# Gathering the dilated patterns' outputs in six transfers instead of 24, and a key projection moved among the fills of the last dilated pass

## What is computed

```python
y_a = dense_attention(...)        # A: latent attention, 4 heads
y_b = dense_attention(...)        # B: grouped-query attention
for gi, (w, r) in enumerate(((128, 1), (512, 4), (2048, 16))):
    o, lse = dilated_group(cq5[:, :, gi], ck5[:, :, gi], cv5[:, :, gi], r, w // (2 * r), dil_bias[gi])
    outs.append(o); lses.append(lse)
alpha = softmax(stack(lses), axis=0)
y_c = sum(alpha[..., None] * stack(outs), axis=0)     # C: dilated, 3 patterns combined per position
y_d = banded_attention(d_q, d_k, d_v, 128, 128, win_bias, sink)   # D: windowed
y = concatenate([y_a, y_b, y_c, y_d]) * silu(gate_path)
x = x + sum(sigmoid(merge_logits) * (y per branch @ w_branch), axis=2) @ w_out
```

## Time and profile before

| | us |
|---|---|
| median of three runs | 2906.52 (2903.6 to 2906.72) |
| the profiled execution | 2898.05 |
| its span, first to last instruction | 2895.9 |
| PE busy | 2720.7 (94%) |
| DVE busy | 1310.1 (45%) |
| ACT busy | 1022.5 (35%) |
| POOL busy | 724.5 (25%) |
| chain that ended last, PE's share | 83% |
| mean granted TensorE clock | 0.98 of full speed |

### The profile page before, as it was taken

How to read it: one execution, slowest core, us unless ns; L and a number is a source line. 1 busy time by engine, 2 the same in 40 slices (tenths; PEclk the granted TensorE clock), 3 DMA queues, 4 the chain that set the end, 5 groups by cost and what they waited for, 6 DMA issues and landing times.

```text
span 2895.9 us, 36963 instructions
## 1 busy us (share of the span) xinstructions
PE 2720.7 (94%) x13836; PEld 2240.9 (77%) x13836; DVE 1310.1 (45%) x2815; ACT 1022.5 (35%) x2085; POOL 724.5 (25%) x449
## 2 busy tenths in 40 slices
PE   7899999999999989999879999998999999899996
PEld 6677887878888768877776777787888887688875
DVE  3575366522434355523145734585234444455222
ACT  4464116412444425511135631173024443354012
POOL 2100331033434232222220014301333333222231
PEclk9999999999999999999989999999999999999998
DMA  7000210021111221112050011100212113111122
GB/s 241 27 1 10 55 43 19 1 59 45 47 44 41 75 72 30 37 46 95 23 183 15 1 28 46 42 10 10 64 40 52 40 40 103 37 37 37 44 95 80
DMA packets 204194, 146.00 MB, mean 50 GB/s; under 512 B 21688, under 2 KB 187192, under 8 KB 203976
## 3 DMA queue, kind: packets, MB, share of 16 engines
q1 hardware_dynamic: 190188, 137.08, 16.7%
q10 hardware_dynamic: 13824, 6.49, 0.8%
HBM read 124.44 MB, written 27.49 MB: 52 GB/s over the span
## 4 chain that ended last, share of the span: by engine, by line
PE 83%; DVE 9%; ACT 3%; issue 2%; DMA 1%; POOL 1%; SPq 1%; ACTq 0%; POOLq 0%; DVEq 0%; another core or an unknown queue 0%
PE ps L892 21%; PE ps L855 9%; PE ps L856 9%; PE ps L857 9%; PE ps L998 5%; PE ps L1023 4%; PE ps L955 4%; PE ps L956 4%; PE ps L957 4%; PE ps L1071 3%; PE ps L1039 3%; PE ps L1008 2%; DVE pt_slots L1814 2%; PE ps L1000 1%; DVE nm L1650 1%
## 5 line engine op out<-in xcount | busy, mean ns | idle before, releaser
L2051 POOL CAST wh<-wraw 128x1024 fp32r<-128x1024 f32 (+2 forms) x162 | 176.2, 1088 | 2058.8 <-PE ps L857 873.1
L855 PE MATMUL ps<-xh,wh 128*128 128x512 f32 x1120 | 442.1, 395 | 3.0 <-ACT pt_split L1542 2.2
L856 PE MATMUL ps<-xl,wh 128*128 128x512 f32 x1120 | 438.2, 391 | 0.0
L857 PE MATMUL ps<-xh,wl 128*128 128x512 f32 x1120 | 438.1, 391 | 0.0
L2053 POOL TENSOR_TENSOR wl<-wraw,wh 128x1024 fp32r<-128x1024 f32 (+2 forms) x162 | 421.0, 2599 | 13.0
L892 PE MATMUL ps<-xh,wh 128*128 128x512 f32 x864 | 353.9, 410 | 3.1 <-ACT att L1368 1.2
L892 PE MATMUL ps<-xh,wl 128*128 128x512 f32 x864 | 344.4, 399 | 0.0
L892 PE MATMUL ps<-xl,wh 128*128 128x512 f32 x864 | 344.2, 398 | 0.0
L855 PEld LDWEIGHTS ps<-xh,wh 128*128 128x128 f32 x1120 | 212.3, 190 | 47.5 <-ACT pt_split L1542 3.0
L857 PEld LDWEIGHTS ps<-xh,wl 128*128 128x128 f32 x1120 | 211.7, 189 | 44.7
L856 PEld LDWEIGHTS ps<-xl,wh 128*128 128x128 f32 x1120 | 212.1, 189 | 43.2
(11 more groups left out here) (213 smaller groups left out, 4748.1 us busy)
## 6 DMA issues: line engine op xcount, KB each, us to landing
wraw<-in_w_in_dram SPq DMA_DIRECT2D x128, 512.0 KB, 3.9
xres<-acc SPq DMA_DIRECT2D x2, 4096.0 KB, 15.8
toep<-toep_row SPq DMA_DIRECT2D x32, 256.0 KB, 10.7
wraw<-in_w_branch_dram SPq DMA_DIRECT2D x64, 128.0 KB, 3.9
wraw<-in_w_out_dram SPq DMA_DIRECT2D x16, 512.0 KB, 3.7
acc<-xres SPq DMA_DIRECT2D x16, 512.0 KB, 7.7
dil_out<-cst ACTq DMA_DIRECT2D x96, 66.0 KB, 1.6
att<-dil_out SPq DMA_DIRECT2D x48, 132.0 KB, 2.5
```

What stands on the lines that cost most here:

```text
L855: pe.matmul(dst, ah, bh, start=i == 0, stop=False)
L856: pe.matmul(dst, ah, bl, start=False, stop=False)
L857: last = pe.matmul(dst, al, bh, start=False, stop=i == len(ks) - 1)
L2051: inc(pool.tensor_copy(high, raw), w_hi)
```

## The change

The dilated outputs now lie as (pattern, block, head) in `dil[0]`, in `att`, and `dil[1]`, a second buffer `dil_late` over the memory of the old query stacks. `load_groups_outputs(half, groups)` moves one pattern's half in one transfer (528 KB), with a semaphore for each half. Two transfers, patterns 0 and 1 of half 0, are issued at the start of the last pass, after 64 of the 96 stores; the four others after all stores, with no wait for `yn_set`. The two fills of the key projection join the gate fills of the last pass: 8 matmuls a step, and 4 in each of the four steps of the tail. PE's other fills of branch D are put around the transposes in another order, with other banks.

```diff
-        dil = att[:, 0:4 * GROUPS * HEADS * REC].rearrange("p (t g h f) -> p t g h f", t=4, g=GROUPS, h=HEADS)
+        dil = [a.rearrange("p (g t h f) -> p g t h f", g=GROUPS, t=4, h=HEADS)
+               for a in (att[:, 0:4 * GROUPS * HEADS * REC], dil_late[:, :])]
...
-        GATE_PART = 7
+        GATE_PART = 8
+        TAIL_PART = 4
...
-                            fill_bank.append((0, 1, 2, 3, 6, 7)[i % 6])
+                            fill_bank.append((2, 3, 0, 1, 6, 7)[i % 6])
...
-                def load_groups_outputs(half):
-                    for st in range(half * 4, half * 4 + 4):
-                        for g in range(GROUPS):
-                            load(dil[:, st % 4, g, :, :].rearrange("p h f -> p (h f)"),
-                                 dil_out[g, st * P:(st + 1) * P, :], dil_in)
+                def load_groups_outputs(half, groups):
+                    for g in groups:
+                        load(dil[half][:, g, :, :, :].rearrange("p t h f -> p t (h f)"),
+                             dil_out[g, half * HALF:(half + 1) * HALF, :].rearrange("(t p) f -> p t f", p=P), dil_in[half])
...
-                for t in dilated["gate_tiles"] + windowed_tiles[:4]:
+                for t in dilated["gate_tiles"]:
+                    load_tile(t)
+
+                sp.wait_ge(lg_ready, dil_passes[5]["units"][0])
+                for s in dil_stored:
+                    sp.wait_ge(s, DIL_PER_SLOT * 16 * 4 // 6)
+                load_groups_outputs(0, (0, 1))
+                for t in windowed_tiles[:4]:
                     load_tile(t)
...
-                load_groups_outputs(0)
+                load_groups_outputs(0, (2,))
+                load_groups_outputs(1, (2, 0, 1))
                 sp.wait_ge(exp_done, c_u1)
                 load_bias(3)
-                sp.wait_ge(yn_set, 1)
-                load_groups_outputs(1)
...
-                        for j, t in enumerate(p["tiles"][:3]):
+                        def dilated_y(half):
+                            pe.wait_ge(yn_set, half + 1)
+                            for st in range(half * 4, half * 4 + 4):
+                                y_transposes(branches[2]["y"][st], yc[:, half, st % 4, :])
+
+                        for j, t in enumerate(p["tiles"]):
+                            if j == 0:
+                                continue
                             pe.wait_ge(w_split, t + 1)
                             for half in range(2):
                                 fill(p["fill"] + 2 * j + half, t, half)
-
-                        for st in range(ST):
-                            pe.wait_ge(yn_set, st // 4 + 1)
-                            y_transposes(branches[2]["y"][st], yc[:, st // 4, st % 4, :])
+                                if j == 2 and half == 0:
+                                    dilated_y(0)
+                        dilated_y(1)
...
-                                    fills_part(b["gate_fill"], b["gate_tiles"], GATE_PART * i, GATE_PART * (i + 1))
+                                    fills_part(b["gate_fill"], b["gate_tiles"] + keys_tile, GATE_PART * i, GATE_PART * (i + 1))
+                            if n == 2 and s >= u1:
+                                m = GATE_PART * 16 + TAIL_PART * (s - u1)
+                                fills_part(b["gate_fill"], b["gate_tiles"] + keys_tile, m, m + TAIL_PART)
```

More of the change, by code:

```diff
@@ L1874, in _ @@
                         windowed = branches[3]["passes"][0]
+                        for f in range(windowed["fill"], windowed["fill"] + 2):
+                            stack_rests(windowed, f)
                         for half in range(2):
-                            dve.wait_ge(dil_in, 16 * 4 * GROUPS * (half + 1))
+                            dve.wait_ge(dil_in[half], 16 * GROUPS)
                             if half:
```

38 lines of the change are left out of this document (20 added, 18 removed).

## The result

The changed kernel took 2862.2 us (median of four runs, 2860.3 to 2865.1), the kernel before in the same rounds 2905.1 (2901.4 to 2906.7): ratio 0.9855, interval 0.9838 to 0.9872, 42.9 us faster. The changed kernel's profiled execution took 2860.8, the one before 2898.05, so the two profiles can explain 37.2 us.

What follows compares the result with a forecast made beforehand. PE was taken to bound the kernel, busy 94% of the span. Gains of 17.7 and 17.0 us less 2 x (0.5 + 1.6 + 0.3) gave 30 off 2898.05, so 2868; plus 8.5, 2876.5 us, range 2865 to 2894.

Steps and rivals of the forecast that it cites:

- Lock-steps: At the y transposes, two groups of four instead of one of eight: 0.3 us lost a layer.
- the same stop and 0.6: Layer 1 gains as layer 0: the 9.4 us stop, and 0.6 us for three low-clock fill matmuls behind it.
- so PE waits 1.6 us: At the first y, PE asks at 1018.3 and the combination ends at 1019.9: a 1.6 us wait in each layer.
- The split's price: POOL's split of the values' tile beside the first combination costs DVE 2.7 us on top of 8.8 alone.
- the 0.6 for a key copy: The first of POOL's eight key copies may catch one more sum of the first combination, adding 0.6 us.
- The offset: The timed median, 2906.52, lies 8.5 us above the profiled execution; the same was added to the changed kernel's 2868.
- The late first combination: Rival: DVE held up by POOL or shared DMA engines, first y 5.5 us later; 8 us a layer, 2892.5; chance 0.13.
- The low clock: Rival: after the first y's wait, 168 matmuls stay at the low clock, 33 us a layer lost; 2942; chance 0.03.
- The last rival: Keys' weights not split when the 96 gate matmuls end, PE stops inside the last pass; about 2905; chance 0.04.
- each values matmul waits for ACT or DVE with nothing between: Reason given for the last dilated pass's tail taking 6.5 us in layer 0 with PE busy for 2.94.

Runs made afterwards that it cites:

- keys_only: The kernel before with only the key projection moved into the last pass and its tail, loads left as they were: 2904.6 us, ratio 1.0026.
- keys_behind: The changed kernel with the key projection back behind the last pass, seven gate matmuls a step, so the loads alone: 2875.1 us, ratio 0.9924.
- pool_waits: The changed kernel with POOL starting the split of the values' weight tile only after the first combination (yn_set 1): 2864.6 us, ratio 0.9884.
- tail_bare: The changed kernel with the tail's 16 key matmuls put behind the tail's last step: 2864.0 us, ratio 0.9879.
- keys_behind_six: keys_behind with six gate matmuls a step instead of seven and the last sigmoid behind the last exponential: 2867.5 us, ratio 0.9898.
- before_six: The kernel before with six gate matmuls a step instead of seven and the last sigmoid behind the last exponential: 2890.2 us, ratio 0.9974.
- six_after: The changed kernel with all six dilated output transfers issued behind the last store, none early: 2876.3 us, ratio 0.9925.

## Why the prediction was right and wrong

**The bound, and the direction: right.** PE has no gap in the tail, the clock reads 1.00, the stops of 9.38 us are gone, and the gain lies in the place and nearly nowhere else. keys_only and keys_behind show that the chain of loads had set the end.

**The times of layer 0: right, in part by luck.** First query fill at 1001.73 (worked out 1001.8), DVE's first row at 1007.87 (1007.8), one 528 KB transfer in 3.73 us (4.2), the second y at 1037.31 (1038.0). DVE's first row came out by errors that cancel: the last store was issued 0.67 us sooner than worked out (1000.28) and the transfer was 0.47 shorter, but the store landed after 3.76 us, not 2.61.

**The sum, 29.9 for 35.0: three terms were mis-sized.** First, *"Lock-steps ... 0.3 lost"*. The y transposes cost 0.60 + 3.27 us before (1040.67 to 1043.94, after the stop, at the low clock) and 1.48 + 1.43 now. That is a gain of 0.96, so 1.26 more a layer, 2.5 in all. I priced three slow fill matmuls behind the stop but not the three slow groups ahead of them, although the first of them stands in the earlier trace rows. Second, *"the same stop and 0.6"* for layer 1: eight matmuls ran slowly there, 2475.37 to 2478.80, 3.43 us against 8 x 0.2285 = 1.83, so 1.6 instead of 0.6. I had carried layer 0's term over without reading layer 1's rows. Third, *"so PE waits 1.6 us"*: it was 1.15 and 0.20 in the first profile, 0.53 and nothing in the second, 0.77 and nothing in the third. The combination took 11.44 us, not 12.1. The split's price was right (8.66 without POOL, so 2.8, where I had 2.7), but the 0.6 for a key copy didn't come, as the copies began at 1018.30, behind the split. In layer 0 the landing as a whole was no shorter; in layer 1 the store landed 1.0 us sooner than in layer 0 (2.76), which is the rest. That is 0.45 and 1.4. With these, layer 0 comes to 15.3 + 1.26 + 0.45 = 17.0 (16.7 measured) and layer 1 to 14.6 + 1.26 + 1.0 + 1.4 = 18.3 (18.3 measured).

**The offset: wrong, and the larger error.** *"The median of the runs, 2906.52, is 8.5 above it, and the changed kernel will be timed in the same way."* The changed kernel's median lay 1.4 above its profiled execution. And the profiled execution of the kernel before, 2898.05, is exactly what the other four sets read as its median (2897.6 to 2898.8). By the sum against the profile alone, 2868.1, the forecast would have missed by 6; the offset added 8.5 to that. Why one set of the kernel before read 2905 is not settled: it was not seen again. The four later sets ran on four different chips and agree within 1.2 us; which chip the first ran on isn't on record, so a slower chip stays possible, and so does something of that set alone.

**The range: too narrow below.** It allowed for no y wait at all and for a timing as low as the profile, 2865, as if no gain could have been priced too low. Every error in the sum was on that side.

**The rivals.** The late first combination didn't come: PE waited 1.15 us, not 7, and the first of the four transfers took 3.73 us, not 10. The Trainium skill ("SBUF — State Buffer", SBUF: two separate sides) has the port pair as an exclusive lock, and pool_waits agrees for operations on SBUF: both engines' rows get longer beside each other, and short again apart. But POOL's key copies fell behind the combination, so there was less to add than that rival assumed. The low clock did not stay. The last rival, that PE would stop for the keys' weights, fell as well.

**A reason that was half right.** I put down the tail's 6.5 us to "each values matmul waits for ACT or DVE with nothing between". tail_bare and the two kernels with six matmuls a step show that most of it came from the bare last two steps, in which nothing covers ACT's last sigmoid and its table loads. In the changed kernel that sigmoid starts at 988.09 and eight fill matmuls a step last to the end of the pass.

## What to carry to other kernels

Read what a stop costs to its end, in each layer: the wait, then everything that follows at the low clock, small matmuls too. When work fills an engine's gaps between small steps, spread it so that it lasts through the last step, and look at what another engine has to do in the steps left bare; here six matmuls a step instead of seven, with the last sigmoid moved behind the last exponential, gave 7.4 us in the kernel before, without the rest of the change. And where one profiled execution and the median of a few runs disagree, don't carry the difference over as if it were a constant: put both into the range.

## What was not expected of the hardware

- **The same waits don't always bring the same clock.** keys_behind_six and before_six have the same tail on PE, waits of 0.54 to 0.55, 0.92 and 0.36 us, in both layers. Behind it, in layer 0, the granted clock was 0.89 in the first and 1.00 in the second; in layer 1 it was the other way round, 1.00 (2419 to 2427 us) in the first and 0.85 (2424 to 2432 us) in the second. The rows of layer 0, keys_behind_six, then before_six:

```profile
997.00:1005.00 8.00, 8.00 (x33) 6.54 (x32) 1.38 (x2) 1.19 (x2) 0.00 (x0) 0.89 1.09 353
```
```profile
997.00:1005.00 8.00, 8.00 (x37) 6.64 (x36) 0.00 (x0) 0.00 (x0) 0.00 (x0) 1.00 0.98 291
```

  In branch B's end of layer 1, too, a fill behind the same wait of 2.95 us took 0.47 us in the changed kernel and 0.76 in tail_bare.
- **Large transfers side by side move more than I had read.** 512 KB loads and the 12 of 132 KB showed 215 GB/s; in six_after the six of 528 KB moved about 350 to 390 GB/s in slices of 0.4 us, and the first three landed 4.8 us (median) after their issue, where the one that counts in the changed kernel takes 3.7.
- **A collision of DVE and POOL lengthens both rows**: cast 1.04 to 1.98 us, subtraction 2.38 to 3.25, beside sums of 1.23 that took 1.94 and 3.30.
